# Moving the first head's logits of a stick-breaking attention in front of the last projection slot

## The reference

```python
def stick_breaking_attention(q, k, v):
    ...
    scale = 1.0 / math.sqrt(dh)
    ...
        z = jnp.einsum('bhqd,bhkd->bhqk', qblk, kh).astype(jnp.float32) * scale
        mask = ts[None, :] < tq[:, None]
        log_1m = jnp.where(mask, jax.nn.log_sigmoid(-z), 0.0)
        rev = lax.cumsum(log_1m, axis=3, reverse=True)
        log_a = jax.nn.log_sigmoid(z) + (rev - log_1m)
        a = jnp.where(mask, jnp.exp(log_a), 0.0)
        return jnp.einsum('bhqk,bhkd->bhqd', a.astype(vh.dtype), vh)
...
            q = (x @ b_wq[j]).reshape(b, s, N_HEADS, HEAD_DIM)
            mix = stick_breaking_attention(q, k_shared, v_shared) @ b_wo[j]
```

## Time and profile before

| What | us |
|---|---|
| median of 3 executions | 1990.07 |
| lowest and highest | 1989.31, 1991.42 |
| the profiled execution, its time | 1990.25 |
| the profiled execution, span of the core | 1988.5 |

### The profile page before, as it was taken

The page is one execution under the profiler, slowest core; times in us unless marked ns, Lnnn a source line. Parts: engine busy times, 40 slices in busy tenths (PEclk is TensorE's granted clock), DMA queues, the critical chain, the costliest instruction groups (busy, mean ns, idle before and its releaser), DMA issues.

```text
span 1988.5 us, 23270 instructions
## 1 busy us (share of the span) xinstructions
PE 1903.7 (96%) x9212; PEld 1533.1 (77%) x9212; DVE 1056.2 (53%) x1274; ACT 765.7 (39%) x987; POOL 173.6 (9%) x123
## 2 busy tenths in 40 slices
PE   6999999999999997999999999899899999999996
PEld 4767788877788665888888888788777888888885
DVE  6874442245445787745555543642676545555434
ACT  5532332245334455442322222542673622222223
POOL 5500000000001354110000000200000200000001
PEclk8999999999999998999999999999899999999998
DMA  9211223211222453123232333133002123232321
GB/s 392 85 64 64 85 85 105 98 51 43 78 91 85 130 151 118 64 85 105 86 105 84 106 106 106 64 106 106 1 1 96 64 85 105 84 105 87 125 88 61
DMA packets 31052, 186.45 MB, mean 94 GB/s; under 512 B 3329, under 2 KB 5505, under 8 KB 10498
## 3 DMA queue, kind: packets, MB, share of 16 engines
q1 hardware_dynamic: 29392, 175.96, 26.2%
q10 hardware_dynamic: 1586, 9.44, 1.2%
HBM read 174.64 MB, written 2.10 MB: 89 GB/s over the span
## 4 chain that ended last, share of the span: by engine, by line
PE 89%; ACT 4%; DVE 3%; issue 2%; DMA 1%; POOL 1%; ACTq 0%; DVEq 0%
PE PS L578 25%; PE PS L580 24%; PE PS L579 24%; PE PS L1081 2%; PE PS L968 2%; PE PS L644 1%; PE PS L646 1%; PE PS L645 1%; PE PS L937 1%; DMA RAW<-w 1%; PE PS L918 1%; PE PS L1055 1%; ACT WH L1127 1%; PE PS L1058 1%; PE PS L1092 1%
## 5 line engine op out<-in xcount | busy, mean ns | idle before, releaser
L578 PE MATMUL PS<-H,WH 128*128 128x512 f32 (+1 forms) x1616 | 625.0, 387 | 26.6 <-POOL L L444 13.5
L580 PE MATMUL PS<-H,WL 128*128 128x512 f32 (+1 forms) x1616 | 617.9, 382 | 0.0
L579 PE MATMUL PS<-L,WH 128*128 128x512 f32 (+1 forms) x1616 | 617.6, 382 | 0.0
L1683 DVE TENSOR_TENSOR WL<-RAW,WH 128x2048 fp32r<-128x2048 f32 x136 | 314.2, 2311 | 269.1 <-ACT WH L1127 264.8
L578 PEld LDWEIGHTS PS<-H,WH 128*128 128x128 f32 x1616 | 305.8, 189 | 98.2 <-issue 18.6
L1127 ACT ACTIVATE WH<-RAW 128x2048 fp32r<-128x2048 f32 x144 | 274.7, 1908 | 225.1 <-PE PS L580 184.3
L580 PEld LDWEIGHTS PS<-H,WL 128*128 128x128 f32 x1616 | 305.7, 189 | 59.4
L579 PEld LDWEIGHTS PS<-L,WH 128*128 128x128 f32 x1616 | 305.8, 189 | 56.7 <-issue 0.5
L444 POOL TENSOR_TENSOR L<-X,H 128x512 fp32r<-128x512 f32 x32 | 46.6, 1464 | 1309.8 <-ACT H L1493 751.5
L1562 ACT ACTIVATE TT<-TT 128x512 f32<-128x512 f32 x44 | 27.8, 632 | 310.4 <-DVE TT L2336 310.4
L578 PE MATMUL PS<-FH,WH 128*128 128x512 f32 (+1 forms) x376 | 142.8, 380 | 0.0
(11 more groups left out here) (341 smaller groups left out, 2485.3 us busy)
## 6 DMA issues: line engine op xcount, KB each, us to landing
RAW<-w SPq DMA_DIRECT2D x148, 1024.0 KB, 4.9
HS<-HC SPq DMA_DIRECT2D x32, 264.0 KB, 5.0
ADA<-w_ada ACTq DMA_DIRECT2D x4, 1024.0 KB, 23.8
ADA<-w_ada SPq DMA_DIRECT2D x4, 1024.0 KB, 23.3
GA<-w_gate SPq DMA_DIRECT2D x1, 4096.0 KB, 17.9
PWR<-w_ple ACTq DMA_DIRECT2D x2, 1024.0 KB, 5.0
out<-X SPq DMA_DIRECT2D x8, 256.0 KB, 2.1
X<-x_t SPq DMA_DIRECT2D x2, 512.0 KB, 6.8
```

The lines of the kernel that those rows point to most:

```text
L578: nc.tensor.matmul(ps, wh, xh, start=start, stop=False, skip_group_check=skip)
L579: nc.tensor.matmul(ps, wh, xl, start=False, stop=False, skip_group_check=skip)
L580: return nc.tensor.matmul(ps, wl, xh, start=False, stop=stop, skip_group_check=skip)
L1683: v.tensor_tensor(WL[:, p], RAW[:, p], WH[:, p].bitcast(F32), ALU.subtract).then_inc(w_lo, 1)
```

## The change

It has five parts.

1. `token_major` takes a function that it calls in front of the last slot of the stage. For `v1` this is `zs(0)`, so that the 12 logit matmuls of head 0 stand before the last slot and no longer behind it. `zs(0)` now waits until group 0 has been copied out (`bank_free` at `GROUP0["v1"] + 1`), and `zs(1)` waits for a new semaphore, `tok_free`, which the copy of the third bank of group 1 raises.
2. The bank sets are swapped: even heads use banks 4 to 6, odd heads banks 0 to 2 (`sb_bank`).
3. On ACT the table load and the softplus of head 0 stand in front of the four copies of group 1. They also wait for `w_lo` to count the last slot of `v1`, because the softplus writes a new name, `EXS`, which lies over that slot's `RAW` buffer.
4. On DVE head 0 uses `EXS` and a high part `EXHS` at a place that no longer holds anything. Its low part still goes over `L`, so DVE waits for the end of the last slot (`slot_done`) before it.
5. SP waits until both pieces of that low part are written (`sp_lo` at 2) before it loads the second slot of `wo` into the buffer of `EXS`.

```diff
+        EXS = at("EXS", 48 + 8 * ((SLOT0["v1"] + COUNT["v1"] - 1) % 2), [P, SBC])
+        EXHS = at("EXHS", 192, [P, SBC], F32R)
...
+        def sb_bank(h):
+
+            b = 4 * ((h + 1) % 2)
+            return PS[:, b:b + 3, :].rearrange("p b t -> p (b t)")
...
-            loads(SLOT0["pw2"] + 2, NSLOTS)
+            loads(SLOT0["pw2"] + 2, SLOT0["wo"] + 1)
+            sp.wait_ge(sp_lo, 2)
+            loads(SLOT0["wo"] + 1, NSLOTS)
...
-            def token_major(stage):
+            def token_major(stage, before_last=lambda: None):
...
+                    if j == COUNT[stage] - 1:
+                        before_last()
                     pe.wait_ge(w_lo, SLOT0[stage] + j + 1)
...
                 if h == 0:
-                    pe.wait_ge(bank_free, GROUP0["v1"] + V_GROUPS)
+                    pe.wait_ge(bank_free, GROUP0["v1"] + 1)
+                if h == 1:
+                    pe.wait_ge(tok_free, 1)
...
+            token_major("v1", lambda: zs(0))
...
-                for ex, ready in ((EXH[h % 2], sp_hi), (EXL[h % 2], sp_lo)):
+                for ex, ready in ((EXH[h % 2] if h else EXHS, sp_hi), (EXL[h % 2], sp_lo)):
...
             for i in range(SB_HEADS + 2):
-                if i < SB_HEADS:
+                if 1 <= i < SB_HEADS:
                     zs(i)
...
-            def v_copy(stage, vtok, group):
+            def v_copy(stage, vtok, group, before_last=lambda: None):
...
+                    else:
+                        before_last()
                     for c in range(NT):
...
+                        if stage == "v1" and g == 1 and c == NT - 2:
+                            ins.then_inc(tok_free, 1)
...
+            def soft(i):
+                ex = EX[i % 2] if i else EXS
+                act.wait_ge(sz_ps, i + 1)
+                if i >= 2:
+                    act.wait_ge(sp_lo, 2 * i - 2)
+                own.did(a(ex[:], sb_bank(i)[:, 0:SBC], ACT.Exp))
+                own.settle()
+                for cc in SB_PARTS:
+                    a(ex[:, cc], ex[:, cc], ACT.Ln, bias=1.0).then_inc(sz_exp, 1)
+
+            def soft_first():
+                tables("natural_log_exp_and_others")
+                act.wait_ge(w_lo, SLOT0["v1"] + COUNT["v1"])
+                soft(0)
...
-                        v.tensor_copy(EXH[i % 2][:, cc], ex[:, cc]).then_inc(sp_hi, 1)
+                        v.tensor_copy(exh[:, cc], ex[:, cc]).then_inc(sp_hi, 1)
+                    if i == 0:
+                        dve.wait_ge(slot_done, SLOT0["v1"] + COUNT["v1"])
```

More of the change, by code:

```diff
@@ L349, in build @@
             "sz_ps", "sz_exp", "sp_ready", "sp_hi", "sp_lo"))
+        tok_free = sem("tok_free")
         tri_done, a_ready, sb_pv = (sem(s) for s in ("tri_done", "a_ready", "sb_pv"))
@@ L1047, in zs @@
                 if h == 0:
-                    pe.wait_ge(bank_free, GROUP0["v1"] + V_GROUPS)
+                    pe.wait_ge(bank_free, GROUP0["v1"] + 1)
+                if h == 1:
+                    pe.wait_ge(tok_free, 1)
                 if h >= 2:
                     pe.wait_ge(a_ready, h - 1)
-                flat = PS[:, 4 * (h % 2):4 * (h % 2) + 3, :].rearrange("p b t -> p (b t)")
+                flat = sb_bank(h)
                 order = (0, 1, 3, 2)
@@ L1614, in _ @@
             act.wait_ge(bank_free, GROUP0["v1"])
-            slots("v1", v_copy("v1", VTOK, V_GROUPS), head=COUNT["v1"])
-            tables("natural_log_exp_and_others")
+            def soft(i):
[11 more added lines that the diff above has]
+                soft(0)
+            v1_copy = v_copy("v1", VTOK, V_GROUPS, soft_first)
+            for j in range(COUNT["v1"]):
+                split_hi(Step(j), 1, SLOT0["v1"] + 1)
+                v1_copy(Step(j), 0)
             def weights(h):
-                flat = PS[:, 4 * (h % 2):4 * (h % 2) + 3, :].rearrange("p b t -> p (b t)")[:, 0:SBC]
+                flat = sb_bank(h)[:, 0:SBC]
                 act.wait_ge(tri_done, h + 1)
@@ L1633, in _ @@
             for i in range(SB_HEADS + 2):
[L1634 to L1643, removed]
+                if 1 <= i < SB_HEADS:
+                    soft(i)
                 if 1 <= i <= SB_HEADS:
@@ L2384, in _ @@
                 if i < SB_HEADS:
-                    flat = PS[:, 4 * (i % 2):4 * (i % 2) + 3, :].rearrange("p b t -> p (b t)")[:, 0:SBC]
-                    ex = EX[i % 2]
+                    flat = sb_bank(i)[:, 0:SBC]
+                    ex, exh = (EX[i % 2], EXH[i % 2]) if i else (EXS, EXHS)
                     if i >= 2:
@@ L2393, in _ @@
                         dve.wait_ge(sp_ready, 2 * i + n + 1)
-                        v.tensor_copy(EXH[i % 2][:, cc], ex[:, cc]).then_inc(sp_hi, 1)
+                        v.tensor_copy(exh[:, cc], ex[:, cc]).then_inc(sp_hi, 1)
+                    if i == 0:
+                        dve.wait_ge(slot_done, SLOT0["v1"] + COUNT["v1"])
                     for n, cc in enumerate(SB_PARTS):
                         dve.wait_ge(sp_hi, 2 * i + n + 1)
-                        v.tensor_tensor(EXL[i % 2][:, cc], ex[:, cc], EXH[i % 2][:, cc].bitcast(F32),
+                        v.tensor_tensor(EXL[i % 2][:, cc], ex[:, cc], exh[:, cc].bitcast(F32),
                                         ALU.subtract).then_inc(sp_lo, 1)
```

1 line of the change is left out of this document (removed).

## The result

The changed kernel takes 1984.62 us, the median of 7 executions (1982.58 to 1985.99), against 1991.37 us of the kernel before in the same comparison (7 executions, 1989.31 to 1992.12). The ratio is 0.9967 with a 95% interval of 0.9958 to 0.9976, so 6.6 us less, 5 to 8. The forecast was 7.35 us less and 1982.7 us; the range of 1981 to 1988 holds the result. Two more comparisons of the same code gave 0.9973 (0.9963 to 0.9983) and, with one semaphore replaced by another, 0.9970 (0.9960 to 0.9979).

The account below looks back on a forecast made before the run. PE was taken to bound the kernel as one long matmul chain, busy 1903.7 of 1988.5 us. Shorter waits of 2.89 us plus 4.46 us of clock gave 7.35 us less, 1990.07 to 1982.7 us; range 1981 to 1988.

Parts of the forecast that it names:

- Parts 2 to 5: Bank swap, ACT's softplus ahead of the copies, DVE's wait, SP's later load: none was to lengthen the path.
- the covers: Slack before `tri(0)` needs the high part (7.4 us), before `zs(1)` needs `tok_free` (2.07), before `EXL` is needed (1.7).
- the signs named: Expected in the new profile: given start times, no PE waits, full clock from 1395 to 1410, 91.04 us from `zs(3)` to `wo`.
- The waits: Start of the attention: shorter PE pauses bring `zs(3)` from 1408.53 at full clock to 1405.64, 2.89 us.
- the bound given: `zs` between two projection slots: cost taken as 0, unknown put at -0.2 (overlap) to +0.7 us.
- The clock: Start of the attention: low PE clock behind the pauses delays `zs(3)` from 1408.53 to 1412.99; 4.46 us to be won.
- the first rival: Start of the attention: clock falls all the same at a remaining pause, gain only 2.89 us, 1987.2 us; chance 0.15.
- My row: Pause of 1.33 us before `zs(3)` at 1412.99 with full clock from 1411, read as the clock staying up: gain 7.35 us.
- The second rival: End of the attention: clock falls there instead, costing about 5 us, 1987.8 us; chance 0.09.
- The fall at both ends: Clock falls at the attention's end while the start keeps its own fall: slower, 1992.3 us; chance 0.05.

Follow-up runs that it names:

- the filled kernel: Kernel before with unread matmuls in all five places where PE pauses, start and end of the attention: ratio 0.9981, T to `zs(4)` 34.48 us.
- the filled kernels: Kernel before or changed kernel with unread matmuls put into some or all PE pauses around the attention: ratios 0.9957 to 0.9991.
- the changed kernel with two pauses filled: Changed kernel plus five unread matmuls before `zs(2)` and five before `zs(3)`: ratio to the kernel before 0.9958.
- the first step alone: Changed kernel with table load and softplus of head 0 again behind the four copies, logits still ahead of the slot: ratio to the kernel before 1.0005.
- the three kernels with some of their pauses filled: Unread matmuls added: kernel before, first pause (0.9991); kernel before, three start pauses (0.9977); changed kernel, pauses before `zs(2)` and `zs(3)` (0.9958).
- first pause filled: Kernel before plus eight unread matmuls between `zs(1)` and `tri(0)`, in the pause of 2.02 us: ratio 0.9991.

## Why the prediction was right, and where it was not

**The order of events.** Taken from T, the forecast against the trace: exponential of head 0 at 3.21 us (1383.9 - 1380.69), measured 1385.35 - 1382.13 = 3.22. `zs(1)` at 12.67, measured 12.49. `zs(2)` at 18.81, measured 18.51. `zs(3)` at 24.95, measured 24.66. `zs(4)` at 31.09, measured 32.35. From `zs(4)` to `wo` 84.90 us before, 84.89 after. Parts 2 to 5 cost nothing, as said: the covers were counted as 7.4, 2.07 and 1.7 us and measured as 7.32 (to the first piece of the high part, as the forecast counted), 1.92 and 1.41 us. Of the signs named, two failed, and both by the clock: it was not full from 1395 to 1410, and from `zs(3)` to `wo` are 1499.37 - 1406.79 = 92.58 us and not 91.04.

**The waits: 2.89 us forecast, 3.65 us measured.** The term that was too small is the time of the kernel before at the full clock. I took 2.95 us for `tri(0)` from the steady loop. With its pauses filled the kernel before shows 3.42 us, since DVE delivers head 0's parts only just in time: the row of the first half has 1.82 us and not 1.57 in the profile of before, too, and the low part is begun only at 1398.95, after `tri(0)` itself. That is 0.47 us. The rest is overlap: `zs(0)` between two slots and `zs(1)` cost 0.18 and 0.12 us less than assumed, 0.30 together, where the bound given was 0.2.

**The clock: 4.46 us forecast, 3.96 us there to be had, 1.52 us of it not won.** The 4.46 were read against the too short path above; with 3.42 us for `tri(0)` it is 3.99, and the filled kernel gives 38.44 - 34.48 = 3.96. The step that failed is the one that kept the full 4.46 us in the sum, on the ground that "1.33 us did not do it at 1412.99". In the changed kernel the clock fell behind one of the pauses of 1.33 us in each of three profiles. So the first rival came about, but at a third of its price, because the clock stayed low for 3.4 us and not ten. 3.65 + 3.96 - 1.52 = 6.09 us is the stretch. The Trainium skill, page "TensorE: Matmul & The Clock Gate", section "A second HAM failure mode: psum-queue depth-cycling", has the clock swing in short idle times between groups of matmuls: on this the traces agree with it, with a fall behind a pause of 1.33 us in three profiles of three. My row did not bear the weight I put on it: in it the clock had only just come back (0.82 from 1410 to 1411, 1.00 from 1411 to 1412), and the pause before that, also of 1.33 us, lay where the clock was low already. One pause without a fall is no proof that pauses of this length are safe. That the forecast still came near is in part luck: the waits gave 0.76 us more than counted, and the clock 2.02 us less.

**The second rival**, a fall at the end of the attention, came in two of the filled kernels. It cost 1.6 us, not 5.1. The low stretch lay on the 16 value matmuls alone (0.59 from 1495.60 to 1499.70 in the changed kernel with two pauses filled, so low for some 3.4 us), and the clock was back before the pause behind them. The fall at both ends, which was to make the kernel slower, was never seen in the changed kernel, and at the prices measured, 1.5 + 1.6 us, it would not have: 6.09 - 1.6 us would still be gained.

**The absolute time.** 1984.62 is 1.9 us above the forecast. Before itself came out at 1991.37 rather than 1990.07 us, which is 1.3 us of it. The other 0.6 us is less than the interval can tell; the stretch, which is exact to some hundredths, is 7.35 - 6.09 = 1.26 us short of the forecast. For the profiled execution: 1981.15 + 1.44 (T later) + 1.26 (31.09 against 32.35) = 1983.85, measured 1983.9.

## What to carry to other kernels

At a hand-over from a dense stage to a chain over several engines, put the first step of the chain and everything that follows it on the other engines beside the last dense piece; the first step alone won nothing here. Count a pause of PE twice, once for the wait and once for the clock behind it. A pause that can't be removed can be filled with matmuls into a free bank (0.26 to 0.29 us each here), but look at the pauses nearby as well: in two of the three kernels with some of their pauses filled the clock fell behind one that was left.

## What the runs showed of the hardware

The clock fell behind pauses of 1.33 us, and in the same kernels did not fall behind pauses of 1.33, 1.49 and 2.23 us. With the same code it fell near 500 us in one execution and not in another. The length of a pause alone does not say whether it falls, and what does besides was not settled. Once low, it stayed so for about 3.4 us (changed kernel), 6.6 us (first pause filled, from 1410 to 1417 on average at 0.53) or 10 us (before).

```profile
1410.00:1417.00 7.00, 7.00 (x31) 6.35 (x32) 4.33 (x8) 2.60 (x3) 0.00 (x0) 0.53 0.00 0
```

The table load took 1.28 us, and the next activation started 1.29 us after it did (1384.06, 1385.35). The Trainium skill, page "ScalarE: Activation LUTs", section "What ACT_TABLE_LOAD costs", counts about 1380 ns of drain on top, 2.66 us for a switch. No row here shows that drain, and the measurement decides.
